# Lower weights first and pair sums in the first expert stage, negation on ScalarE, rows spread anew, and the last two value blocks together

## The reference, cut to what matters

```python
v1, i1 = lax.top_k(s[:, :, 0], PEER_TOPK); v2, i2 = lax.top_k(s[:, :, 1], PEER_TOPK)   # routing
best, j = lax.top_k(cand, PEER_TOPK)
gate = jax.nn.softmax(best, axis=-1)
...
u_sel = expert_u[ec]                                    # 16,384 experts x 2048
a = jax.nn.gelu(jnp.einsum('cd,chkd->chk', tc, u_sel))
w = gc * a
return jnp.einsum('chk,chkd->cd', w, expert_v[ec])      # 16,384 experts x 2048
```

## Time and profile before

| what | value |
|---|---|
| median of 3 runs | 1981.88 us (1981.82 to 1983.32) |
| the profiled execution's own time | 1982.32 us |
| its span | 1980.4 us |
| PE, PE weight load, DVE, ACT, POOL busy | 1951.8, 1736.4, 1687.4, 1124.5, 722.7 us |
| upward stage, by PE's first L838 and first L861 | 784.5 to 1383.8 us |
| value stage with the last block | 1383.8 to 1973.2 us |
| granted TensorE clock in both | 1.00 |

### The profile page before, as it was taken

How to read it: one execution, slowest core, us unless ns; L and a number is a source line. 1 busy time by engine, 2 the same in 40 slices (tenths; PEclk the granted TensorE clock), 3 DMA queues, 4 the chain that set the end, 5 groups by cost and what they waited for, 6 DMA issues and landing times. The chain is left out here.

```text
span 1980.4 us, 32655 instructions
## 1 busy us (share of the span) xinstructions
PE 1951.8 (99%) x11696; PEld 1736.4 (88%) x11696; DVE 1687.4 (85%) x2446; ACT 1124.5 (57%) x1633; POOL 722.7 (36%) x406
## 2 busy tenths in 40 slices
PE   8999999999999999999999999999999999999998
PEld 7999989998888888999999999999777777777776
DVE  6877777776878777999999999998888888888897
ACT  7565556555676455566565655655454555555554
POOL 0301110111000001888888888885222221223220
PEclk9999999999999999999999999999999999999999
DMA  5755654566455556999999999999999999999997
GB/s 211 251 175 192 195 195 159 191 201 199 151 177 183 186 181 222 316 324 323 322 326 317 328 322 339 350 403 380 331 379 370 370 372 386 372 379 376 378 367 241
DMA packets 137576, 566.50 MB, mean 286 GB/s; under 512 B 44008, under 2 KB 52080, under 8 KB 88112
## 3 DMA queue, kind: packets, MB, share of 16 engines
q1 hardware_dynamic: 87440, 414.83, 57.8%
q0 software_dynamic: 49776, 148.44, 22.3%
q10 hardware_dynamic: 304, 2.62, 0.4%
HBM read 548.30 MB, written 16.88 MB: 285 GB/s over the span
## 5 line engine op out<-in xcount | busy, mean ns | idle before, releaser
L450 DVE TENSOR_TENSOR wlo<-raw,whi 128x1024 fp32r<-128x1024 f32 x242 | 295.9, 1231 | 113.7 <-PE psum L588 71.0
L838 PE MATMUL psum<-xr,whi 128*128 128x384 f32 x2048 | 380.8, 337 | 0.0
L861 PE MATMUL psum<-whi,xr 128*128 128x512 f32 x1524 | 367.4, 390 | 2.4 <-DVE xr L1742 1.3
L838 PEld LDWEIGHTS psum<-xr,whi 128*128 128x128 f32 x2048 | 351.1, 188 | 0.3
L861 PEld LDWEIGHTS psum<-whi,xr 128*128 128x128 f32 x1524 | 285.5, 188 | 65.1 <-DVE xr L1742 1.9
L584 PE MATMUL psum<-xr,whi 128*128 128x512 f32 x1312 | 336.1, 398 | 5.6 <-issue 4.3
L459 ACT ACTIVATE whi<-raw 128x2048 fp32r<-128x2048 f32 (+1 forms) x170 | 322.9, 1900 | 30.1 <-DMA raw<-v_rows 18.7
L443 ACT ACTIVATE whi<-raw 128x1024 fp32r<-128x1024 f32 x244 | 249.9, 1053 | 100.1 <-PE psum L574 42.7
L1283 POOL DMA_INDIRECT arena<-v_rows,small x64 | 145.9, 2280 | 403.4 <-DVE arena L1706 401.3
L584 PEld LDWEIGHTS psum<-xr,whi 128*128 128x128 f32 x1312 | 236.1, 189 | 51.2 <-issue 5.1
L1288 POOL DMA_INDIRECT gates<-arena x96 | 206.2, 2147 | 29.3 <-issue 29.3
(11 more groups left out here) (278 smaller groups left out, 3242.8 us busy)
## 6 DMA issues: line engine op xcount, KB each, us to landing
raw<-stream SPq DMA_DIRECT2D x244, 512.0 KB, 3.3
raw<-v_rows SPq DMA_DIRECT2D x85, 1024.0 KB
raw<-u_cols SPq DMA_DIRECT2D x84, 1024.0 KB
arena<-v_rows SPq DMA_DIRECT2D x43, 1024.0 KB
arena<-u_cols SPq DMA_DIRECT2D x42, 1024.0 KB
gates<-arena POOLq DMA_DIRECT2D x8, 1536.0 KB, 9.7
small<-gates SPq DMA_DIRECT2D x62, 192.0 KB
arena<-x_t SPq DMA_DIRECT2D x4, 544.0 KB, 7.5
```

The costliest lines, as they stand in the source:

```text
L450: nc.vector.tensor_tensor(wlo[:, k % 2 * HALF:(k % 2 + 1) * HALF], raw[:, s * HALF:(s + 1) * HALF], f(whi[:, s * HALF:(s + 1) * HALF]), AL ...
L838: mm(bank(at, 0, 2 * TD), hi_w[:, c * P:(c + 1) * P], z_all[:, :, c, 0:TD // TS, :], start=c == 0, stop=False)
L861: last = mm(at[:, (b * 4 + j * 2 + n) * 512:(b * 4 + j * 2 + n + 1) * 512], weights, src, start=begin, stop=end, skip_group_check=True)
```

## The change

- `hi_block(n+2)` moves ahead in ACT's order: it now waits for PE's upper products of block n (a new semaphore, `upper_free`) and for the lower split of n, not for all products of n. In the last turn it stands before the weights' upper part and the low copy.
- DVE does `lo_block(n+1)` first in block n, and always as one instruction of 2048 columns (before, the last 24 blocks had two halves). `lo_block(128)` stands before the first gates.
- `expert_sums` and `gelus` handle two blocks at once, every second block.
- The negation of the best score moves from DVE (L1669) to ACT.
- Row product n is at step 6 + 9n/2 (before 6 + 22n/5) for n < 46, then 211 + 5(n-46)/2 (before 207 + 27(n-46)/10). By the formulas of POOL's order this puts gather 63 behind all 192 scatters (before: behind 190).
- The last two value blocks are multiplied together, first banks 4 to 7 of both, then bank by bank 0 to 3 with six products each. Block 127's parts get buffers of their own. The moves of residuals and of the sparse sum come one block earlier. SP stores the low rows and banks 0 to 2, ACT stores bank 3.

```diff
         def row_at(n):
             if n < 46:
-                return 6 + n * 22 // 5
+                return 6 + n * 9 // 2
             if n < ROWS:
-                return 207 + (n - 46) * 27 // 10
+                return 211 + (n - 46) * 5 // 2
...
-            split = LO_SPLIT <= b < B_U or b == B_U + B_V - 1
...
+            nc.vector.tensor_tensor(lows[b % 2], *halves, ALU.subtract).then_inc(lo_done, 2)
...
-            for n in range(4):
+            def store_bank(n):
                 sp.wait_ge(out_sb, n + 1)
...
+            store_low(0)
+            store_bank(0)
+            store_low(1)
+            store_bank(1)
+            store_bank(2)
...
+                last.then_inc(upper_free, 1)
+                pe.wait_ge(lo_done, base * 2 + 2 * b + 2)
...
+            for q, c in enumerate(last_two):
                 pe.wait_ge(w_hi, c + 1)
...
+                for j in range(2):
+                    last = lower_rows(q, j)
+                    if q:
                         last.then_inc(low_products, 1)
...
+            for n in range(4):
+                pe.wait_ge(residual_in, n + 1)
+                for q in range(2):
+                    add(bank(n), Whi[q][:, 0:P], hi_w[q][n])
+                    add(bank(n), Wlo[q][:, 0:P], hi_w[q][n])
+                    last = add(bank(n), Whi[q][:, 0:P], lo_w[q][n], q == 1)
+                last.then_inc(last_products, 1)
...
+                ch.link(A(neg_best, best[:, 0:1], ACT.Copy, scale=-1.0))
...
+            def gelus(n):
+                act.wait_ge(bank_free, F_U + n + 4)
+                A(W[:, n:n + 2, :], W[:, n:n + 2, :], ACT.Gelu)
...
             for n in range(B_U):
+                act.wait_ge(upper_free, n + 1)
+                act.wait_ge(lo_done, 2 * F_U + 2 * n + 2)
+                hi_block(act, n + 2)
                 if n == B_U - 1:
                     weight_hi(0, 0)
                 act.wait_ge(half_done, 2 * F_U + 2 * n + 2)
...
-                hi_block(act, n + 2)
-                if n:
-                    gelu(n - 1)
+                if n and n % 2 == 0:
+                    gelus(n - 2)
...
+            act.wait_ge(out_sb, 4)
+            act.dma_start(out[0:P, 3 * 512:], arena[:, 3 * 512:4 * 512]).then_inc(stored, 16)
...
+            def expert_sums(n):
+                dve.wait_ge(half_done, 2 * F_U + 2 * n + 4)
+                dve.wait_ge(low_part, n + 2)
+                both = psum[:, U_BANKS[n % 4] * 512:(U_BANKS[n % 4] + 2) * 512].rearrange("p (b t) -> p b t", b=2)
+                V.tensor_tensor(W[:, n:n + 2, :], both[:, :, 0:TD], W[:, n:n + 2, :], ALU.add).then_inc(bank_free, 2)
 
             for n in range(B_U):
-                if n:
-                    expert_sum(n - 1)
+                lo_block(dve, n + 1)
+                if n and n % 2 == 0:
+                    expert_sums(n - 2)
                 step(2 * n)
                 step(2 * n + 1)
-                if n < B_U - 1:
-                    lo_block(dve, n + 1)
-                if n == B_U - 2:
-                    gate_weights(0)
+            gate_weights(0)
+            expert_sums(B_U - 2)
             weight_lo(0)
-            expert_sum(B_U - 1)
-            lo_block(dve, B_U)
             gate_weights(1)
```

More of the change, by code:

```diff
@@ L341, in hybrid_layer @@
         ROUTES = 2 * HEADS
-        LO_SPLIT = B_U - 24
         SUMMED = KC - 3
@@ L455, in hi_block, with last_hi_half, last_lo_half @@
             act.wait_ge(block_landed[b % 3], 16 * (b // 3 + (b % 3 == 2)))
[L456 to L460, removed]
+            nc.scalar.activation(whi[:, b % 2 * D:(b % 2 + 1) * D], slots[b % 3], ACT.Copy).then_inc(hi_done, 2)
         def lo_block(dve, b):
[L463 to L464 removed]
+            dve.wait_ge(hi_done, 2 * F_U + 2 * b + 2)
             dve.wait_ge(half_done, 2 * F_U + 2 * b - 2)
             halves = [t.rearrange("p (z n) -> p z n", z=2) for t in (slots[b % 3], f(whi[:, b % 2 * D:(b % 2 + 1) * D]))]
[L467 to L473, removed]
+            nc.vector.tensor_tensor(lows[b % 2], *halves, ALU.subtract).then_inc(lo_done, 2)
+        B_LAST = B_U + B_V - 1
+        def last_hi_half(act, z):
+            act.wait_ge(block_landed[B_LAST % 3], 16 * (B_LAST // 3 + (B_LAST % 3 == 2)))
+            nc.scalar.activation(last_hi[:, z * HALF:(z + 1) * HALF], slots[B_LAST % 3][:, z * HALF:(z + 1) * HALF],
+                                 ACT.Copy).then_inc(hi_done, 1)
+        def last_lo_half(dve, z):
+            at = slice(z * HALF, (z + 1) * HALF)
+            dve.wait_ge(hi_done, 2 * F_U + 2 * B_LAST + z + 1)
+            nc.vector.tensor_tensor(last_lo[:, at], slots[B_LAST % 3][:, at], f(last_hi[:, at]), ALU.subtract).then_inc(lo_done, 1)
         @block.sync
@@ L895, in _ @@
             value_block(0, 1, False)
-            with pe.Fori(0, B_V // 2 - 3) as i:
+            with pe.Fori(0, B_V // 2 - 4) as i:
                 for q in range(2):
                     value_block(i * 2, 2 + q, False)
[L899 to L906, removed]
+            value_block(0, B_V - 6, False)
@@ new lines, in _, with add @@
+            value_block(0, B_V - 5, False, idle=0)
+            value_block(0, B_V - 4, False, idle=1, residual=0)
+            value_block(0, B_V - 3, False, residual=1)
+            last_two = (B_V - 2, B_V - 1)
+            hi_w = [[t[:, n * 512:(n + 1) * 512] for n in range(4)] for t in (whi[:, 0:D], last_hi)]
+            lo_w = [[lows[0][:, n // 2, n % 2 * 512:(n % 2 + 1) * 512] for n in range(4)],
+                    [last_lo[:, n * 512:(n + 1) * 512] for n in range(4)]]
+            def add(at, weights, src, last=False):
+                return mm(at, weights, src, start=False, stop=last, skip_group_check=True)
@@ new lines, in lower_rows @@
+            def lower_rows(q, j):
+                c = last_two[q]
+                pe.wait_ge(hi_done, 2 * F_V + 2 * c + (j + 1 if q else 2))
+                for n in (2 * j, 2 * j + 1):
+                    add(bank(4 + n), Wboth[q], hi_w[q][n])
+                pe.wait_ge(lo_done, 2 * F_V + 2 * c + (j + 1 if q else 2))
+                for n in (2 * j, 2 * j + 1):
+                    last = add(psum[0:TS, (4 + n) * 512:(5 + n) * 512], Whi[q][:, P:TD], lo_w[q][n], q == 1)
+                return last
```

79 lines of the change are left out of this document (35 added, 44 removed).

## The result

| | kernel before | changed kernel |
|---|---|---|
| median on the same chip | 1981.85 us (4 runs) | 1997.72 us (4 runs, 1996.06 to 1999.87) |
| ratio, 95% interval | 1 | 1.0076 (1.0063 to 1.0089) |
| profiled execution, its span | 1982.32, 1980.4 us | 1999.87, 1997.9 us |
| upward stage | 784.5 to 1383.8 us | 785.6 to 1399.7 us |
| value stage, to PE's last product | 589.4 us | 594.3 us |

The change makes the kernel 15.9 us slower by the medians; 1974.9 was forecast. The profiled execution is the slowest of the four, its span 17.5 us longer, and its parts show where: the value stage starts 15.9 us later (1.1 of it lie before the upward stage) and takes 4.9 longer, and from ACT's last copy on it is 2.9 shorter.

The account below looks back on a forecast made before the run. DVE sets the upward stage's pace; after the change POOL's queue sets its end. Span 1980.4 - 5.0 (value stage's start) - 2.0 (end) = 1973.4; + 1.9 - 0.4 gives 1974.9 us, range 1967 to 1987.

Parts of the forecast that it names:

- POOL falls behind: slower: Rival, gather 63 to row product 63: gather 63 at 1377.5, value stage +9.0 us, 1988.9 us in all; chance 0.17.
- deciding point: End of the upward stage: the slower rival holds once gather 63 starts after 1372.5, value stage +2.0 us.
- the sum for gather 63: POOL's queue, late upward stage: 1360.3 + 3.7 + 4.5 - 3 = 1365.5, bounds 1351 and 1377.5.
- (b): Last 23 upward splits, now whole, delay POOL by 0 to +9.9 us; +4.5 taken, an even beat locking less.
- (a): POOL's queue: two more scatters go before gather 63, 2 x 1.87 = +3.7 us.
- (c): Upward stage: faster blocks let POOL gain up to 10 us or lose 3.6; -3 taken.
- DVE's work: Upward stage from block 8: pair sums, negation moved and one row product less save 6 to 9 of 11.3 us.
- Order: Upward stage: earlier splits allow 2.5 us more lateness, once; 0 to 2.8 us of stall remain, 1 taken.
- (d): POOL's 3.6 us of waits for row products go if POOL is late, 0 to -3.3 us; 0 taken.
- From gather 63 to the value stage: Seam: issue, landing (6 us taken), row product 63, split, gates, weights and handing over, 13.3 us; value stage at 1378.8.
- Rows in mid-stage: Upward stage: PE stalling in mid-stage for rows was named as a sign of being wrong; no size given.
- The end: Last two value blocks and stores: earlier, spread stores gain between 0 and 3.0 us; -2.0 taken.

Follow-up runs that it names:

- experiment 3: Changed kernel, splits whole, with row products back at the old steps (22/5 and 27/10): 1985.88 us, ratio 1.0019.
- experiment 13: Kernel before with the new end, pair sums and negation on ACT, but the old engine order, halves and rows: 1981.72 us, ratio 0.9993.
- experiments 8: Changed kernel with the last 24 splits halved and old rows, except the last 18 row products 2.5 steps apart from step 207: 1982.73 us, ratio 0.9997.
- experiment 10: Kernel of experiment 8 with the first weights and first gate product put first in the last upward turn: 1976.78 us, ratio 0.9975.
- experiment 12: Kernel of experiment 10 with ACT's low copy of block 127 before the upper part of block 129: 1976.42 us, ratio 0.9969.
- experiment 4: Kernel before with only the last 24 upward lower splits made whole instead of halves: 1993.66 us, ratio 1.0065.
- experiment 7: Kernel before with only the change's new end, measured on two chips: 1980.58 us, ratio 0.9997, and 1980.56 us, ratio 0.999.
- experiment 9: Changed kernel with the last 24 splits halved, old rows, and weights and gate product first in the last upward turn: 1978.53 us, ratio 0.9987.
- experiment 11: Changed kernel with only the weights and gate product put first in the last upward turn: 1998.55 us, ratio 1.0078.
- experiment 1: Changed kernel with only the lower splits of the last 24 upward blocks in halves again: 1983.1 us, ratio 1.0011.

## Why the prediction was wrong

The mechanism I had as a rival ("POOL falls behind: slower", 0.17) is what happened, and it went beyond its own bound. Its deciding point, gather 63 after 1372.5, held. The step that failed is the sum for gather 63: 1365.5 forecast, at most 1377.5, measured 1386.5. That is 21.0 us, and the value stage is 1399.7 - 1378.8 = 20.9 late. Two of its terms were too small, the whole splits (b) and what the rows' new steps do to POOL's last stretch, of which only (a) was counted; and (c) had the wrong sign.

- **DVE's work.** Forecast 6 to 9 us of 11.3, measured 4.2. The pair sum was priced right: it takes 0.550 us and holds DVE for 0.47 (1393.88 to 1394.34), forecast 0.48. What didn't show is the row product less in this stretch, 2.3 us: with the old rows experiment 3 has 4.638 us a block and experiment 13 4.645. Experiment 13 shows that pair sums and negation bring all of the 4.2.
- **Order.** Forecast: more room for DVE, nothing for ACT. Blocks 8 to 101 gained no more with the new order than without (4.650, 4.645). Its price is ACT's wait for block loads, 93.3 us where it was 14.1. In mid-stage little comes of it: DVE's splits wait 8.3 us in all for ACT's upper parts, where they waited 3.8. At the seam weights and the low copy stand behind it: PE's stops of 4.63 and 4.67 us in experiments 8 and 10 hang on it, and that of experiment 10 shrank to 0.63 in experiment 12. In time neither step is clear of the noise (ratios 0.9997, 0.9975, 0.9969, each interval overlapping the next).
- **(a) Two more scatters, +3.7.** Not measured alone. It is part of what the rows' new steps cost: 11 us of time in experiment 3, and there gather 63 is 13.8 us earlier. The changed kernel has 20 gathers and 40 scatters to do after 1253 us, where the kernel before had 18 and 37, and so has experiment 3. That moving row products by up to four steps loads POOL's last stretch is a term that I left out.
- **(b) Whole splits, +4.5 of at most 9.9.** This step failed. Experiment 4 isolates it: gather 63 at 1377.1, +16.7. Delays in that stretch are 113.3 - 37 x 1.56 - 17 x 1.00 = 38.6 us, over 27 splits 1.4 each, where halves had 0.77; I took 1.0 and at most 1.2, the value of the first stretch, where routing still lies between splits and row products. That routing makes the difference isn't shown. I wrote that an even beat should lock less by chance; in the rows of experiment 4 each split catches a scatter. The bound left out a second thing: with POOL late the stretch is longer, and 27 splits fell into it, not 23.
- **(c) Faster blocks, -3.** Wrong in sign: in the first stretch POOL's delays grew from 122 to 128.9 us and it did 4 operations less. I had noticed two operations per block and priced it as a gain. With whole splits it is about all that POOL did in any stretch here, and the last one had 2.2 before.
- **(d)** POOL's waits did go, -3.3, which I had set to 0.
- **From gather 63 to the value stage, 13.3.** Measured 13.2, and that is luck in part. Landing took 6.3 us for this gather (forecast 6; the median is 8.8), but it wasn't what row product 63 waited for: DVE came to it 7.9 us after the issue, behind row products 61 and 62.
- **Rows in mid-stage.** I had looked at row product 63 alone. The late gathers stopped PE from block 110 on already.
- **The price in clock.** Not foreseen: 1.8 us in the first value block, and 3.4 behind the two long gaps before the seam. Of the 4.9 us that the value stage is longer, the 1.8 and the 0.9 at the last two blocks explain 2.7. The other 2.2 lie between, in a few blocks that take longer than 4.57 us: in the changed kernel 5.3 and 5.5 us for those that start at 1779.0 and 1784.3, in which ACT waits 2.6 and 3.2 us for block loads, and 6.0 for the one at 1812.8. The kernel before has such blocks too (6.5 us at 1407.4), and whether the change makes them more no run shows.
- **The end, -2.0.** Right by the trace: 2.9 us gained in the stores, 0.9 given back by PE in the last two blocks. By time it isn't shown: ratios 0.9997 and 0.999 in experiment 7, and both intervals reach 1.

## What to carry to other kernels

Before making an instruction longer, look at who works in its seams: here a split cut in two cost 0.06 us more on VectorE, and whole it cost 12 us through GpSimd. An engine that never rests has only so many operations per block; compare that with what each stretch of the schedule needs, not with the average. When work is moved ahead of something in a queue, read what the moved instruction waits for at the seam of two stages, where the next stage's loads are not there yet.

## What was unexpected of the hardware

- GpSimd's indirect DMAs and VectorE's splits can fall into step: a scatter that starts 0.6 us into a 2.29 us split takes 3.1 instead of 1.56 us, and in experiment 4 the next scatter meets the next split at the same place.
- A stop of TensorE can cost more than the wait itself, by the lower clock behind it. It did so after 3.65 and 4.67 us (granted 0.64 over 7.1 us; ten products 4.64 us instead of 2.56), but also after 2.62 and 3.90 us (0.73 over 6.3), and after 1.75 us in experiment 9 and 1.90 in experiment 11 (0.73 again: 16 lower products 3.17 and 3.35 us instead of 1.92). It did not after 2.42 us in experiment 1 and 2.60 in experiment 3, where the products behind went at full speed. So the length of the stop alone doesn't decide it. Where it happened it cost 1.7 us (0.27 x 6.3) to 2.6 us (0.36 x 7.1).
- A gather of 1 MB took 8.8 us from issue to landing (median of 64), with the DMA share at 0.94 to 0.98.
